# o's inverse norms to rows: both transfers begun by SyncE instead of ScalarE

## The reference

```python
def _rmsnorm(x, g):
    xf = x.astype(jnp.float32)
    y = xf * lax.rsqrt(jnp.mean(xf * xf, axis=-1, keepdims=True) + EPS)
    return (y * g.astype(jnp.float32)).astype(x.dtype)
...
p = jax.nn.softmax(sc, axis=-1)
a = p[:, :, 0] - lam * p[:, :, 1]
return jnp.einsum('bhqk,bkhe->bqhe', a.astype(v.dtype), v)
...
o = _rmsnorm(o, subln) * (1.0 - lambda_init)
return o.reshape(b, s, V_WIDTH) @ w_o
```

## Time and profile before

| | |
|---|---|
| median of three runs | 941.27 us (940.96 to 941.45) |
| profiled execution | 941.54 us |
| its span, first to last instruction | 939.7 us |
| busy: PE, PEld, DVE | 934.1, 771.6, 683.8 us |
| busy: ACT, POOL | 470.7, 89.8 us |
| transfers | 130.45 MB, mean 139 GB/s |
| stage of the heads | from about 386 to 580 us of the span |

### The profile page before, as it was taken

How to read it: one execution, slowest core, us unless ns; L and a number is a source line. 1 busy time by engine, 2 the same in 40 slices (tenths; PEclk the granted TensorE clock), 3 DMA queues, 4 the chain that set the end, 5 groups by cost and what they waited for, 6 DMA issues and landing times.

```text
span 939.7 us, 11721 instructions
## 1 busy us (share of the span) xinstructions
PE 934.1 (99%) x4439; PEld 771.6 (82%) x4439; DVE 683.8 (73%) x989; ACT 470.7 (50%) x614; POOL 89.8 (10%) x70
## 2 busy tenths in 40 slices
PE   9999999999999999999999999999999999999998
PEld 7888888888888888888888887888888888888887
DVE  6876766676676689988887886757766676667685
ACT  7644343333434438787777773535334333433441
POOL 3000000100000002123222220000100000010010
PEclk9999999999999999999999999999999999999999
DMA  7328682494556644233333232336485458248535
GB/s 258 105 90 239 153 234 90 99 264 129 135 142 173 179 85 120 71 107 93 102 103 103 90 101 90 90 91 188 126 248 155 122 121 250 90 92 225 175 90 135
DMA packets 101583, 130.45 MB, mean 139 GB/s; under 512 B 4297, under 2 KB 63481, under 8 KB 101537
## 3 DMA queue, kind: packets, MB, share of 16 engines
q1 hardware_dynamic: 85632, 98.31, 32.0%
q0 software_dynamic: 14080, 29.91, 17.5%
q10 hardware_dynamic: 1824, 1.61, 0.7%
HBM read 127.69 MB, written 4.75 MB: 141 GB/s over the span
## 4 chain that ended last, share of the span: by engine, by line
PE 91%; DVE 4%; ACT 2%; DMA 2%; issue 1%; SPq 0%; ACTq 0%; DVEq 0%
PE bank L1695 28%; PE bank L1697 28%; PE bank L1696 28%; PE bank L1967 2%; PE bank L1957 1%; DMA raw<-in_w_mlp_out_dram 1%; DVE w_low L1080 1%; PE bank L1996 1%; DMA work<-in_x_dram 1%; PE bank L1872 1%; DVE a_low_buf L1163 0%; ACT w_high L729 0%; ACT w_high L666 0%; PE bank L1938 0%; PE bank L1806 0%
## 5 line engine op out<-in xcount | busy, mean ns | idle before, releaser
L1695 PE MATMUL bank<-h_high_buf,w_high 128*128 128x512 f32 x640 | 252.2, 394 | 0.0
L1697 PE MATMUL bank<-h_high_buf,w_low 128*128 128x512 f32 x640 | 249.5, 390 | 0.0
L1696 PE MATMUL bank<-h_low_buf,w_high 128*128 128x512 f32 x640 | 249.1, 389 | 0.0
L1695 PE MATMUL bank<-w_high,a_high_buf 128*128 128x512 f32 (+1 forms) x452 | 176.1, 390 | 0.1
L1697 PE MATMUL bank<-w_high,a_low_buf 128*128 128x512 f32 (+1 forms) x452 | 175.1, 387 | 0.0
L1696 PE MATMUL bank<-w_low,a_high_buf 128*128 128x512 f32 (+1 forms) x452 | 175.1, 387 | 0.0
L1080 DVE TENSOR_TENSOR w_low<-raw,w_high 128x2048 fp32r<-128x2048 f32 (+2 forms) x56 | 120.3, 2148 | 51.4 <-ACT w_high L729 31.8
L1695 PEld LDWEIGHTS bank<-h_high_buf,w_high 128*128 128x128 f32 x640 | 120.2, 188 | 26.5 <-issue 2.2
L1697 PEld LDWEIGHTS bank<-h_high_buf,w_low 128*128 128x128 f32 x640 | 120.1, 188 | 25.5
L1696 PEld LDWEIGHTS bank<-h_low_buf,w_high 128*128 128x128 f32 x640 | 120.3, 188 | 24.1
L738 ACT ACTIVATE work<-work 128x512 f32<-128x512 f32 x64 | 40.0, 632 | 177.9 <-DVE work L1147 177.9
(11 more groups left out here) (187 smaller groups left out, 1162.5 us busy)
## 6 DMA issues: line engine op xcount, KB each, us to landing
raw<-in_w_mlp_out_dram SPq DMA_DIRECT2D x24, 1024.0 KB, 6.8
raw<-in_w_mlp_out_dram POOLq DMA_DIRECT2D x24, 1024.0 KB, 8.5
raw<-in_w_mlp_in_dram SPq DMA_DIRECT2D x16, 1024.0 KB, 6.2
work<-in_w_mlp_out_dram SPq DMA_DIRECT2D x8, 1024.0 KB, 5.1
work<-in_w_mlp_in_dram SPq DMA_DIRECT2D x8, 1024.0 KB, 7.6
raw<-in_w_kv_dram SPq DMA_DIRECT2D x16, 512.0 KB, 4.0
xT<-in_w_mlp_out_dram SPq DMA_DIRECT2D x8, 1024.0 KB, 4.8
xT<-in_w_mlp_in_dram SPq DMA_DIRECT2D x8, 1024.0 KB, 7.0
```

Of the source, the lines that this page charges most:

```text
L1695: pe.matmul(acc, w_hi, m_hi, start=start, stop=False, skip_group_check=onto)
L1696: pe.matmul(acc, w_hi, m_lo, start=False, stop=False, skip_group_check=onto)
L1697: return pe.matmul(acc, w_lo, m_hi, start=False, stop=stop, skip_group_check=onto)
```

## The change

The store and the load leave ACT's order of work. SP begins both, in a new function `spread_o_row(m)`, which waits for the inverse norms, begins the store, waits for its landing, waits (from m = 1 on) for the earlier head's o to be multiplied, and begins the load. It stands in SP's order behind the three weight transfers of head m + 3; for m = 5 it stands behind the second unit of w_o's weights. SP's loop over the heads is divided for this into heads 0 to 2, head 3 alone and heads 4 to 7. ACT's waits for the earlier landing and for the earlier o go too. DVE's wait before it overwrites `o_rstd_buf` is now for the earlier row's landing instead of its store.

```diff
--- before.py
+++ after.py
@@ -530,12 +530,29 @@
 
             load_mlp(0)
 
-            with sp.Fori(0, H) as n:
+            def load_head(n):
                 slot_free(U_HEAD + 2 * n)
                 sp.dma_start(tile3(raw[1][:, 0:1024], KC), wk_v[:, :, bass.ds(n * P, P)]).then_inc(w_landed[1], 16)
                 sp.dma_start(tile3(raw[1][:, 1024:2048], KC), wq_v[:, :, bass.ds(n * P, P)]).then_inc(w_landed[1], 16)
                 slot_free(U_HEAD + 1 + 2 * n)
                 sp.dma_start(tile3(raw[0][:, 0:1024], KC), wk_v[:, :, bass.ds(D + n * P, P)]).then_inc(w_landed[0], 16)
+
+            def spread_o_row(m):
+
+                sp.wait_ge(o_inverse, m + 1)
+                sp.dma_start(o_row.rearrange("(p i) -> p i", p=P), o_rstd_buf[:, :]).then_inc(o_row_stored, 16)
+                sp.wait_ge(o_row_stored, 16 * m + 16)
+                if not isinstance(m, int) or m > 0:
+                    sp.wait_ge(o_ready, m)
+                sp.dma_start(o_rstd_bc, o_row.rearrange("(a n) -> a n", a=1).to_broadcast([P, S])).then_inc(o_row_landed, 16)
+
+            with sp.Fori(0, 3) as n:
+                load_head(n)
+            load_head(3)
+            spread_o_row(0)
+            with sp.Fori(4, H) as n:
+                load_head(n)
+                spread_o_row(n - 3)
             for f in range(NF):
                 for q in range(2):
                     u = U_WO + 2 * f + q
@@ -547,6 +564,8 @@
                     else:
                         sp.dma_start(tile3(raw[u % 2], 4), wo_v[:, 4 * q:4 * q + 4, f * S:(f + 1) * S])\
                           .then_inc(w_landed[u % 2], 16)
+                    if u == U_WO + 1:
+                        spread_o_row(H - 3)
             load_mlp(1)
 
             for p, half, f in ((P2, 0, 0), (P3, 0, 1), (P7, 1, 1), (P4, 1, 0)):
@@ -928,16 +947,6 @@
                 dst = o_all[:, h, :] if isinstance(h, int) else o_all[:, bass.ds(h, 1), :]
                 act.activation(dst, b[:, :], ACT.Copy).then_inc(o_copied, 1)
 
-            def store_o_row(m):
-
-                act.wait_ge(o_inverse, m + 1)
-                act.dma_start(o_row.rearrange("(p i) -> p i", p=P), o_rstd_buf[:, :]).then_inc(o_row_stored, 16)
-
-            def load_o_row(m):
-
-                act.wait_ge(o_row_stored, 16 * m + 16)
-                act.dma_start(o_rstd_bc, o_row.rearrange("(a n) -> a n", a=1).to_broadcast([P, S])).then_inc(o_row_landed, 16)
-
             def o_high(k):
 
                 act.wait_ge(o_ready, k + 1)
@@ -1016,18 +1025,12 @@
                 bias_scale(n, (0, 1))
                 bring_table(ACT.Exp)
                 k_high(n)
-                if not second:
-                    act.wait_ge(o_row_landed, 16 * h - 16)
-                store_o_row(h - 1)
                 bias_scale(n, (2, 3))
                 split_high_rest(U_HEAD + 2 + 2 * n)
                 if last:
                     o_high(1)
                 o_copies(h, I[3])
                 o_squares(h, I[3])
-                if not second:
-                    act.wait_ge(o_ready, h - 1)
-                load_o_row(h - 1)
 
             first_head()
             head(1, second=True)
@@ -1611,7 +1614,7 @@
                 kq_inverses(n)
                 if not first:
                     if not second:
-                        dve.wait_ge(o_row_stored, 16 * h - 16)
+                        dve.wait_ge(o_row_landed, 16 * h - 16)
                     o_inverses(h - 1)
                 at_lows(h)
                 k_norm(n, I[0])
```

## The result

The changed kernel took 947.34 us, the median of 6 runs (945.85 to 947.62). The kernel before took 941.57 us, with its runs beside these (6 runs, 940.96 to 942.36). The ratio is 1.0058 with a 95% interval of 1.0045 to 1.0071: it is slower by 0.6%, some 5.8 us. The forecast was no change.

A forecast was written before the change was run, and what follows sets the result against it. PE was taken as the bound, busy 934.1 of 939.7 us. Loads 0.00, stores 0 to -0.24 (-0.04 likely) and SP 0.00 took the median 941.27 to 941.2 us, range 940.4 to 942.2.

The forecast's parts named there:

- Where the 0.04 us goes: ACT in a loop head: the store's saved 0.04 us joins 0.57 us of idle time; PE gains 0.04 or nothing.
- the sum: Whole kernel: 0.00 from the loads, 0 to -0.24 us from the stores (-0.04 likely), 0.00 on SP.
- signs of being wrong: Head distance moving 0.3 us or more; PE waiting on ACT's squares or ACT on weights; PE's time changing outside the heads.
- theory B: From the experiments, not the prediction: DVE is slowed through SP, by the row's load starting or landing differently, or SP's queue.
- the sentence that it cited: Skill's DMA page: beginning transfers from another engine saves only sequencer time; by it alone, twelve issues would give 3.9 us.
- Neither rival: Faster: PE follows ACT's sequencer, 3.9 us saved, 937.3 us, chance 0.03. Slower: weights late behind SP's store, 945.3, chance 0.03.
- The slower one (SP held at the store): SP's wait for the store's landing delays weights; ACT late above 11.2 us landing; at 12 us, 945.3 us; chance 0.03.
- The range: Whole kernel: 940.4 to 942.2 us, around a forecast of 941.2.
- the 0.94 for no change: Whole kernel: chance 0.94 of no measurable difference, mostly within half a us of 941.2.
- the stores' 0.24: Six stores on ACT: 0.24 us saved if each one's 0.04 us reached PE.

The follow-up runs named there:

- The spare store: Changed kernel, SP doing both transfers, plus a 2 KB store nobody needs begun by ACT where the old store stood; 945.51 us, ratio 1.0037.

## Why the prediction was wrong, point by point

The times put on the small steps were right. The store cost ACT 0.03 us at its next instruction, for which 0.04 was forecast, and 0.05 at the high part of the weights, a spacing that the forecast didn't compare. The load cost nothing that shows. SP issued the store 0.03 us after the inverses were ready (475.74 + 0.17, 475.94), the row when the earlier o was ready (478.79 + 1.09 = 479.88, issued 479.95), and k's weights 0.22 us after their release. The row landed in 3.2 us, so about 483.2 and before the weights left at 485.54. The swapped wait of DVE, the divided loop and the queue cost nothing: the kernel with only the load moved shows it, at a ratio of 0.9999, and the one in which POOL waits shows it for both transfers, at 0.9995.

The step that failed is "Where the 0.04 us goes". It followed the saving along ACT alone, through L893 and L684 to the pause before the copy of o, and called it absorbed there. L684 is also what releases POOL, and the prediction didn't follow that release: what an earlier POOL does to DVE had no term in the sum. POOL's subtraction was nearly simultaneous with DVE's scalings in every loop head, and the order of the two had a price of 2.15 us on DVE, of which 1.25 reached PE. The sum had 0 to -0.24 us for the stores; it was +5.0. Of the signs of being wrong that the prediction named, the first came: the distance between heads moved by more than 0.3 us.

The trace of the kernel before held the warning. Its subtractions at L604 had two lengths, 2.38 to 2.42 us where DVE's scalings were over before POOL began, and 2.69 to 2.70 in the four loop heads, where both fell together. This is the one of head 1:

```profile
431.03 2.38 POOL L604 TENSOR_TENSOR w_low<-raw,w_high 128x1024 fp32r<-128x1024 f32 x1 [6.16 <-ACT w_high L684]
```

An instruction of the same shape that takes 0.3 us more beside another engine is a sign of a shared resource.

The Trainium skill describes this one. Its page "SBUF — State Buffer", section "Who interferes with whom", says that VectorE and GpSimd share one pair of SBUF ports as an exclusive lock, that VectorE's tensor_scalar, the operation of the scalings, can enter a mode that uses this pair too, and that of such an operation and one of GpSimd the later one waits until the earlier has ended. The traces agree in the points that they can show: 2.63 us instead of 0.49 for a scaling behind POOL, 0.3 us more for POOL behind a scaling, and no effect on the scaling of v, which has one operand in PSUM. In which mode the scalings ran, no trace here shows. The page also says that ScalarE never waits on anyone and that transfers don't contend with the engines, which fits the failure of theory B. The prediction drew on this skill's rules for transfers only, and the sentence that it cited is on time of the sequencer: the twelve issues did leave ACT's sequencer, and no time of the kernel came of it.

Neither rival named it. The slower one (SP held at the store) stands at its threshold of 11.2 us for a landing, with 2.7 us the longest measured; it played no part. The range and the 0.94 for no change were too sure. They were put together from the stores' 0.24 and the spread of the runs, and no row was asked how much later DVE, which PE follows at the scores, may be. It was about 0.9 us (2.15 on DVE less 1.25 on PE).

What stays open: that the ports are the shared resource is the page's statement; the runs show the exclusion and which operations here it meets, not the wires. Each kernel was profiled in one execution. That an operation of DVE with two SBUF operands is kept out by POOL was not seen, since k_low started first where they met. Measured and profiled losses, 5.8 and 6.1 us, exceed the 5.0 of the four heads. In the profiled pair the rest is at the start: head 0's scalings began 1.06 us later (408.93 against 407.87), and at 408.1 to 408.8 in the profiled executions of the other kernels. In the medians it is 0.7 us, which no trace assigns. The two kernels that show the same loss by other edits lost 5.1 and 5.5 us. No kernel tried was measurably faster than the kernel before.

## What to carry to other kernels

When an engine gets faster off the critical path, follow everything that it releases, not only its own next instruction: each engine that starts sooner may get ahead of another at a shared resource. Look for instructions of one shape with two durations, since here the exclusion showed up as duration and not as waiting, and check how many hundredths of a us separate the two starts. Where an order matters, write it down, by a wait or by moving the short operation ahead of the long one; a kernel that has the good order by 0.02 to 0.03 us, like the one before, has it by luck.

## What was not expected of the hardware

Starts 0.31 and 0.33 us behind DVE's first scaling (307 and 328 ns in one execution) decided over 2.15 us on DVE and 1.25 us of the whole, head by head within one execution. A store's issue of 0.33 us on ACT's sequencer moved the engine by 0.03 to 0.05 us in the kernel before. The spare store, which has the same size and shape, moved it by 0.02 in one head and not at all in three. Taking twelve issues off ACT's queue cost 0.6%.
